# A two-block transformer kernel on one core: shorter first norm, other orders of weight splits, and another grouping of the second block's output projection

## What is computed

```python
def first_block(x, mem, ...):
    h = rms_norm(x, g[0])                       # the norm "n0"
    proj = h @ w_in[l]
    y_a = hyena_mixer(...); y_b = neighbourhood_attention(...); y_c = short_conv_mixer(...)
    merged = gates * (y @ w_branch) summed over the three
    x = x + rms_norm(merged @ w_out[l], g[1])   # residual "r1", then norm "n2"
    x = x + rms_norm(memory_cross_attention(...), g[3])        # "r3", then "n4"
    x = x + rms_norm(conv_glu_ffn(h, ffn_up, ffn_conv, ffn_down), g[5])   # "r5", then "n6"

def conv_glu_ffn(h, w_up, w_conv, w_down):
    u = dwconv3(h @ w_up, w_conv)
    g, val = jnp.split(u, 2, axis=-1)
    return (jax.nn.gelu(g, approximate=True) * val) @ w_down

def second_block(x, ...):
    y_a = mla_mixer(...)    # 6 heads, causal, latent queries and keys
    y_b = diff_mixer(...)   # 4 heads, p0 - lam * p1, then a norm over each head
    y_c = swa_mixer(...)    # 6 heads, window of 128
    h = h + jnp.concatenate([y_a, y_b, y_c], axis=-1) @ w_out[l]
    hn = rms_norm_2(h, ffn_norm[l])             # the norm "n8"
    h = h + (silu(hn @ w_gate[l]) * (hn @ w_up[l])) @ w_down[l]
    h = rms_norm_2(h, final_norm)
```

## Time and profile before

| | us |
|---|---|
| median of 3 runs | 1924.4 |
| lowest, highest | 1922.62, 1929.21 |
| the profiled execution, its own time | 1930.18 |
| its span, first to last instruction | 1928.4 |

### The profile page before, as it was taken

How to read it: one execution, slowest core, us unless ns; L and a number is a source line. 1 busy time by engine, 2 the same in 40 slices (tenths; PEclk the granted TensorE clock), 3 DMA queues, 4 the chain that set the end, 5 groups by cost and what they waited for, 6 DMA issues and landing times.

```text
span 1928.4 us, 22192 instructions
## 1 busy us (share of the span) xinstructions
PE 1825.9 (95%) x8955; PEld 1461.8 (76%) x8955; DVE 1016.3 (53%) x1521; ACT 733.0 (38%) x1219; POOL 289.0 (15%) x233
## 2 busy tenths in 40 slices
PE   7899999999999988989999999889978999999998
PEld 5678876788888866777888888777656778888887
DVE  6777844444454466357777722574354644444322
ACT  4433343332334444344344422444355632223221
POOL 1013501011212140141111100500100111111000
PEclk9899999999999999989999999898987999999999
DMA  5222322232224321222232232331210122222221
GB/s 187 84 80 88 110 77 77 77 110 98 95 91 164 132 87 34 72 71 77 88 104 93 77 109 99 107 102 52 79 42 32 45 87 99 98 88 99 92 94 55
DMA packets 49829, 171.13 MB, mean 89 GB/s; under 512 B 5882, under 2 KB 8570, under 8 KB 49600
## 3 DMA queue, kind: packets, MB, share of 16 engines
q1 hardware_dynamic: 45216, 155.69, 24.1%
q0 software_dynamic: 3936, 13.51, 2.1%
q10 hardware_dynamic: 576, 0.52, 0.1%
HBM read 165.51 MB, written 4.19 MB: 88 GB/s over the span
## 4 chain that ended last, share of the span: by engine, by line
PE 80%; DVE 8%; ACT 5%; issue 4%; POOL 2%; DMA 1%; SPq 0%; DVEq 0%; POOLq 0%; ACTq 0%
PE ps L373 25%; PE ps L375 24%; PE ps L374 24%; PE ps L378 3%; PE ps L2563 2%; ACT ws_h L301 1%; DVE ws_l L309 1%; POOL sums L420 1%; PE ps L2580 1%; ACT P L2687 1%; POOL x L1422 1%; DMA x<-in_x 1%; DVE tmp L800 0%; DVE P L2810 0%; ACT PT L2703 0%
## 5 line engine op out<-in xcount | busy, mean ns | idle before, releaser
L309 DVE TENSOR_TENSOR ws_l<-raw,ws_h 128x1024 fp32r<-128x1024 f32 x289 | 392.0, 1361 | 538.2 <-ACT ws_h L301 537.9
L373 PE MATMUL ps<-h_h,ws_h 128*128 128x512 f32 (+1 forms) x1448 | 584.8, 404 | 32.4 <-DVE ws_l L309 13.5
L374 PE MATMUL ps<-h_l,ws_h 128*128 128x512 f32 (+1 forms) x1448 | 573.9, 396 | 0.0
L375 PE MATMUL ps<-h_h,ws_l 128*128 128x512 f32 (+1 forms) x1448 | 573.6, 396 | 0.0
L301 ACT ACTIVATE ws_h<-raw 128x1024 fp32r<-128x1024 f32 x289 | 303.6, 1054 | 462.4 <-PE ps L375 458.4
L373 PEld LDWEIGHTS ps<-h_h,ws_h 128*128 128x128 f32 x1448 | 278.4, 192 | 108.1 <-issue 23.6
L375 PEld LDWEIGHTS ps<-h_h,ws_l 128*128 128x128 f32 x1448 | 278.9, 193 | 62.1
L374 PEld LDWEIGHTS ps<-h_l,ws_h 128*128 128x128 f32 x1448 | 279.8, 193 | 59.1 <-issue 0.2
L373 PE MATMUL ps<-G_h,ws_h 128*128 128x512 f32 (+1 forms) x374 | 143.0, 382 | 1.1 <-DVE ws_l L309 1.1
L375 PE MATMUL ps<-G_h,ws_l 128*128 128x512 f32 (+1 forms) x374 | 142.6, 381 | 0.0
L374 PE MATMUL ps<-G_l,ws_h 128*128 128x512 f32 (+1 forms) x374 | 142.6, 381 | 0.0
(11 more groups left out here) (437 smaller groups left out, 2425.3 us busy)
## 6 DMA issues: line engine op xcount, KB each, us to landing
raw<-in_ffn_up SPq DMA_DIRECT2D x88, 512.0 KB, 3.3
raw<-in_w_merge SPq DMA_DIRECT2D x36, 512.0 KB, 3.4
raw<-in_ffn_down SPq DMA_DIRECT2D x22, 512.0 KB, 3.4
raw<-in_w_down SPq DMA_DIRECT2D x22, 512.0 KB, 3.3
raw<-in_w_hy SPq DMA_DIRECT2D x12, 512.0 KB, 4.6
raw<-in_w_sc SPq DMA_DIRECT2D x12, 512.0 KB, 3.3
raw<-in_fwd SPq DMA_DIRECT2D x8, 512.0 KB, 3.4
raw<-in_w_naqk SPq DMA_DIRECT2D x8, 512.0 KB, 3.2
```

Source lines behind the costliest of these rows:

```text
L309: dve.e.tensor_tensor(w.lo, raw[n % NRAW][:], w.hi, ALU.subtract).then_inc(*lo_made.says(("lo", n)))
L373: pe.e.matmul(o, a.hi, b.hi, start=start, stop=False, skip_group_check=True)
L374: pe.e.matmul(o, a.hi, b.lo, start=False, stop=False, skip_group_check=True)
L375: return pe.e.matmul(o, a.lo, b.hi, start=False, stop=stop, skip_group_check=True)
```

## The change

It has these parts. (1) n0 uses the form with tokens over the partitions, and POOL adds all six squares; the spread stands on PE behind projection tile 3. (2) In `residual_dve` (r1, r3, r5) the low part of h tile 0 comes one tile sooner. (3) In both feed-forwards one chunk call moves from round 21 to the place between the evacuations of i = 0 and i = 1 in round 2, so that all rounds from 3 on run one chunk further ahead. (4) In `latent_*` the queries of each pair come ahead of its keys, and both ahead of the values; the eight small operations for lambda go to the start of the DVE's stage. (5) The output projection is grouped as k = 0, 1 (`pm`), k = 2, 3 (`pd`) and k = 4 to 7 (after the attention); `pm 0` may start once the last `turn` of M 2 is issued, `pd 0` once `mixed` of D 0 is. (6) `difference` of block 3 of a D pair moves ahead of the next pair's first scores. (7) `out2_*` follows the grouping: 32 blocks in place of 24, four h tiles made early in place of five.

By the planner's rule the D and W pairs get 32 dense steps of three matmuls in place of 40. `pm 0` to `pm 7` stand from the last `turn` of M 2 to the second scores of block 3 of D 1; `pd 0` behind `mixed` of D 0, and `pd 7` behind `over` of W 1, so that W 2 has none (before: `pd 0` behind `mixed` of D 1, `pd 7` behind `over` of W 2).

```diff
@@ -34,8 +34,8 @@
-LAST_PARTS = [(m, k) for m in range(3) for k in (5, 6)] + [(m, 7) for m in range(3)] + [
-    (m, k) for m in range(3, 8) for k in (5, 6, 7)]
+LAST_PARTS = [(m, k) for m in range(2) for k in (4, 5, 6)] + [(m, 7) for m in range(2)] + [
+    (m, k) for m in range(2, 8) for k in (4, 5, 6, 7)]
@@ -579,7 +579,9 @@
                 pe.wait_ge("consts")
-                total("n0", L, bank(("sum", "n0"), main), 8, True)
+                total_of_tokens("n0", bank(("sum", "n0"), main))
+            if m == 3:
+                spread_tokens("n0", bank(("spread", "n0"), main))
             if m == 5:
@@ -697,7 +699,9 @@
             if t == ("hy", 2):
-                root("n0", L, D, rh[:, 0:L])
+                root_of_tokens("n0", D)
+            if t == ("hy", 3):
+                scale_of_tokens("n0", rh[:, 0:L])
             if t == ("hy", 4):
@@ -756,8 +760,6 @@
         sine("f1", 64, 1, "hy_b1", "hy_f1", turns)
-        for m in (2, 4, 6):
-            add_square(dve, added_dve, "n0", m, L)
@@ -769,8 +771,8 @@
                     *dve_part.says(("H", 1)))
-            if t == ("hy", 3):
-                inverse("n0", rh[:, 0:L])
+            if t == ("hy", 2):
+                inverse_of_tokens("n0")
             if t == ("hy", 4):
@@ -904,7 +906,7 @@
         pool.e.dma_start(dec[:], A["decay"]).then_inc(*dec_in.says("dec", by=16))
-        for m in (1, 3, 5):
+        for m in range(1, 7):
             add_square(pool, added_pool, "n0", m, L)
@@ -1403,7 +1405,9 @@
                     *dve_out.says(("rs", v, m), ("off done", v) if off else ("free", (v, m))))
-            if m > 1:
+            if m == 1:
+                h_rest(nv, 0, ngain, dst(0))
+            elif m > 2:
                 h_rest(nv, m - 2, ngain, dst(m - 2))
@@ -1749,6 +1753,8 @@
+
+    UP_CHUNKS = [8, 16, 16] + [16] * 18 + [8, 0]
     UP_LATE = [[] if i < 2 else [0, 1] if i == 2 else [i - 1] for i in range(23)]
@@ -1767,13 +1773,14 @@
         for n in range(23):
-            f.next(8 if n == 0 else 16 if n < 22 else 0)
+            f.next(UP_CHUNKS[n])
             if n == 22:
...
             for i in UP_LATE[n]:
+                f.next(8 if i == 1 else 0)
                 for j in range(2):
@@ -1841,12 +1849,12 @@
     def out2_pe():
-        main, blocks = rings["main"], Blocks("w_out_w", 24)
+        main, blocks = rings["main"], Blocks("w_out_w", 32)
         for m, k in LAST_PARTS:
-            o = bank(("o2", m), main) if k == 5 else out_of(("o2", m))
+            o = bank(("o2", m), main) if k == 4 else out_of(("o2", m))
             w = blocks.next()
             pe.wait_ge(("mix", k))
-            i = mm(o, w, hk(k), k == 5, k == 7)
+            i = mm(o, w, hk(k), k == 4, k == 7)
             what = blocks.says() + ([("done", ("o2", m))] if k == 7 else [])
@@ -1867,11 +1875,11 @@
             squared_x(m)
-            if m < 5:
+            if m < 4:
                 begun(m)
-            if m in (1, 4):
+            if m in (1, 3, 5):
                 f.next(8)
-        for m in range(5, 8):
+        for m in range(4, 8):
             begun(m)
@@ -1879,7 +1887,7 @@
-        return ("done", ("pm", 7) if m < 3 else ("pd", 7) if m < 5 else ("o2", 7))
+        return ("done", ("pm", 7) if m < 2 else ("pd", 7) if m < 4 else ("o2", 7))
@@ -1892,11 +1900,11 @@
             onto_x("o2", m, ("x", "o2", m), ("x", "pd", m))
-            if 1 < m < 7:
+            if 1 < m < 6:
                 h_rest("n8", m - 2, "ffn_norm_2", hm(m - 2))
-            if m in (1, 4):
+            if m in (1, 3, 5):
                 f.next(8)
-        for m in range(5, 8):
+        for m in range(4, 8):
             h_rest("n8", m, "ffn_norm_2", hm(m))
@@ -2091,20 +2101,19 @@
             keys_pe(("dk", m), dblocks)
-        rings["dense"] = dblocks, Blocks("w_swa", 32), Blocks("w_qb", 12), Blocks("w_out_m", 24), Blocks("w_out_d", 16)
+        rings["dense"] = dblocks, Blocks("w_swa", 32), Blocks("w_qb", 12), Blocks("w_out_m", 16), Blocks("w_out_d", 16)
         n = chunk_pe("w_kvb")
         for p in range(2):
+            for t in ("qn", "qr"):
+                o = bank((t, p), main)
+                for k in range(2):
+                    query_part(t, p, k, o)
             for i in range(2):
...
                True).then_inc(*products.says(("done", ("vl", i)), over(n) if i == 4 else None))
-        for p in range(2):
-            for t in ("qn", "qr"):
-                o = bank((t, p), main)
-                for k in range(2):
-                    query_part(t, p, k, o)
@@ -2215,7 +2224,10 @@
         act.e.activation(KW.hi, wsp[n % NSPLIT][:, 0:384].hi, ACT.Copy).then_inc(*act_part.says("KW hi"))
+        fq.next(8)
         for p in range(2):
+            query_hi2("qn", p)
+            query_hi2("qr", p)
             for i in range(2):
@@ -2223,10 +2235,6 @@
                 *act_out.says(("V made2", i), ("free", ("vl", i))))
-        fq.next(8)
-        for p in range(2):
-            query_hi2("qn", p)
-            query_hi2("qr", p)
         act.wait_ge("lam sums")
@@ -2241,6 +2249,17 @@
     def latent_dve():
+        pl = PCOL["lam"]
+        for i in range(2):
+            a, b = small[:, 16 + 16 * i:32 + 16 * i], small[:, 48:64]
+            at = lambda q: par[:, pl + 64 * i + 16 * q:pl + 64 * i + 16 * q + 16]
+            dve.e.tensor_tensor(a, at(0), at(2), ALU.mult).then_inc(*dve_part.says(("lam a", i)))
+            dve.wait_ge(("lam s", i - 1) if i else None)
+            dve.e.tensor_tensor(b, at(1), at(3), ALU.mult).then_inc(*dve_part.says(("lam b", i)))
+            dve.wait_ge(("lam a", i), ("lam b", i))
+            dve.e.tensor_tensor(a, a, b, ALU.add).then_inc(*dve_part.says(("lam s", i)))
+            dve.wait_ge(("lam s", i))
+            dve.e.tensor_reduce(small[:, 2 + i:3 + i], a, AX.X, ALU.add).then_inc(*dve_part.says("lam sums"))
         f = Follow(chunk_dve)
@@ -2294,25 +2313,13 @@
         dve.e.tensor_scalar(KW.lo, wsp[n % NSPLIT][:, 0:384].lo, 1.0, None, ALU.mult).then_inc(*dve_part.says("KW lo"))
-        for p in range(2):
-            for i in range(2):
-                key_lo(p, i)
         fq.next(8)
...
             query_lo2("qr", p)
...
+            for i in range(2):
+                key_lo(p, i)
         dve.wait_ge("lam exp")
@@ -2402,7 +2409,7 @@
     def steps_of(t):
-        return {"sk": 8, "q2": 8, "kn": 1, "qn": 2, "qr": 2, "pm": 3, "pd": 2}[t[0]]
+        return {"sk": 8, "q2": 8, "kn": 1, "qn": 2, "qr": 2, "pm": 2, "pd": 2}[t[0]]
@@ -2468,9 +2475,9 @@
                     break
-                if t == ("pm", 0) and ("mixed", ("M", 2), None) not in said:
+                if t == ("pm", 0) and ("turn", ("M", 2, 3), "meta") not in said:
                     break
-                if t == ("pd", 0) and ("mixed", ("D", 1), None) not in said:
+                if t == ("pd", 0) and ("mixed", ("D", 0), None) not in said:
                     break
@@ -2493,7 +2500,7 @@
                 before = STEPS[at - 1][1]
-                if at and before[0] == "D" and STEPS[at][1] != before:
+                if at and before[0] == "D" and before[2] < 3 and STEPS[at][1] != before:
                     yield "difference", before, None
@@ -2504,6 +2511,8 @@
                 yield "over", u[0:2], None
+            if u[2] == 2 and u[0] == "D":
+                yield "difference", u[0:2] + (3,), None
             if n:
@@ -2631,7 +2640,7 @@
                 blocks = {"q2": dblocks if m < 2 else sblocks, "pm": mblocks, "pd": oblocks}[t[0]]
-                kk = k + (3 if t[0] == "pd" else 0)
+                kk = k + (2 if t[0] == "pd" else 0)
                 if t[0] != "q2":
@@ -3112,8 +3121,8 @@
     wo = wo.reshape(8, 128, 8, 128).transpose(2, 0, 1, 3)
-    A["w_out_m"] = chunks_of(wo[:, 0:3].reshape(-1, 128, 128))
-    A["w_out_d"] = chunks_of(wo[:, 3:5].reshape(-1, 128, 128))
+    A["w_out_m"] = chunks_of(wo[:, 0:2].reshape(-1, 128, 128))
+    A["w_out_d"] = chunks_of(wo[:, 2:4].reshape(-1, 128, 128))
     A["w_out_w"] = chunks_of(np.stack([wo[m, k] for m, k in LAST_PARTS]))
...
     A["ffn_up_2"] = blocks_of(up)
```

20 lines of the change are left out of this document (6 added, 14 removed).

## The result

The changed kernel takes 1917.8 us (median of 20 runs, 1911.2 to 1922.9), the kernel before, on the same chip, 1927.7 us. The ratio is 0.9942 with an interval of 0.9931 to 0.9953, that is -11.2 us (-13.3 to -9.1). It is faster, by about half of the -23.7 us that were forecast. 1917.8 lies inside the stated range of 1888 to 1920, near its slow end; the forecast was 1900.7. The profiled execution took 1918.88 us, its span is 1917.1.

The account below looks back on a forecast made before the run. PE (TensorE), busy 1825.9 of 1928.4 us, bounds the kernel, so only its waits and half-clock stretches count. The terms sum to -23.7 us: 1906.5 us profiled, median 5.8 us below, so 1900.7 us, range 1888 to 1920.

Parts of the forecast that it names:

- (f): Attention: 20 us lost to half clock; 0.3 of it taken back with the longest waits gone; -6, between -12 and 0.
- Part 1: First norm: first tile scaled at 43.4 in place of 45.64, POOL adding all squares; -2.0, between -3.3 and -0.5.
- part 2: r1, r3, r5: low part of first h tile comes sooner, PE waits less; -1.0, between -1.9 and +0.8.
- the first norm doesn't do what it says: Rival: PE's two tiles hold the spread, POOL is slow, first norm at +1, total 1903.7 us; chance 0.05.
- Part 3: First feed-forward, round 2: earlier chunk removes a 4.30 us stall and its clock loss; -7.0, between -7.8 and -3.0.
- Part 4: Latent stage: queries come first, so scores start about 1.3 us sooner; -1.3, between -3.0 and +0.5.
- (b): Attention: two turns wait 7.1 us for difference; the first wait goes whole, 1.8 us of the second stays; -5.3.
- (d): Attention: new wait, DVE stands at pm 0's add until x returns; +2.6, between 0 and +4.
- (a): Attention: pm 0 no longer needs mix 2, for which it waited 4.3 us; -4.3.
- (e): Attention: 8 blocks, 5.6 us, move behind it, half of that counted as cost; +2.8, between 0 and 5.6.
- part 6: End of output projection: PE's 2.2 us wait for a split goes, as DVE keeps up; -2.4, between -2.6 and 0.
- the attention gives nothing: Rival: attention at zero: x's return delays exps, less filler keeps clock down, moved blocks lie bare; 1910.7 us, chance 0.22.

Follow-up runs that it names:

- e1: Kernel before with the change's first norm alone (sum by tokens, POOL adding all six squares): 1929.8 us, ratio 1.0013.
- e2: Kernel before with the chunk call between the evacuations of the two feed-forwards alone: 1925.7 us, ratio 0.9990.
- e11: Kernel before with the reordered latent stage alone (queries ahead of keys and values, lambda's small operations earlier): 1925.5 us, ratio 0.9974.
- e5: Kernel before with the new place of the differences and the regrouped output projection, nothing else: 1922.0 us, ratio 0.9967.
- e4: Kernel before with the new place of the last difference of each D pair alone: 1915.35 us, ratio 0.9935.
- e10: Kernel before with the first norm's sum by tokens, its squares still added by DVE and POOL in turns: 1926.0 us, ratio 0.9985.
- e17: Kernel before with new place of differences and regrouped projection, but M's products starting only behind mixed M 2: 1916.2 us, ratio 0.9946.
- e18: Kernel before with new place of differences and 8 blocks moved behind the attention (M over 3 tiles, D over 1): 1915.2 us, ratio 0.9953.
- e6: Changed kernel with the regrouping of the projection taken back, all other edits kept: 1916.6 us, ratio to the kernel before 0.9937.
- e7: Changed kernel without the regrouping and with the first norm's squares added in turns: 1909.6 us, ratio to the kernel before 0.9904.
- e15: Second measurement of the changed kernel without regrouping, first norm's squares added in turns: 1907.1 us, ratio to the kernel before 0.9904.
- e12: Changed kernel with M over 2 tiles, D over 3, 24 blocks behind, first norm's squares added in turns: 1910.4 us, ratio to before 0.9904.
- after: First measurement and trace of the changed kernel, all edits against the kernel before: 1917.8 us, ratio 0.9942.
- e13: The changed kernel once more, unchanged, with a new profile: 1917.0 us, ratio to the kernel before 0.9957.

## Why the prediction was wrong

The parts as forecast and as measured, alone or in pairs:

| part | forecast | measured | by |
|---|---|---|---|
| 1 first norm | -2.0 | +2.5 (-1.2 to +6.2) | e1 |
| 2 low part sooner | -1.0 | about -0.2 in waits | traces |
| 3 feed-forwards | -7.0 | -1.9 (-5.2 to +1.3) | e2 |
| 4 latent | -1.3 | -5.0 (-8.1 to -1.9) | e11 |
| 5 and 6 attention, projection | -12.4 | -6.4 (-9.8 to -2.9) | e5 |
| sum | -23.7 | -11.0 | change: -11.2 |

**The step that failed first: the clock.** In part 5 it is (f), "with the longest waits gone I take back 0.3 of it, -6". The waits went (28.5 to 21.9 us idle in the last stage), and PE's busy time there rose by 6.1 us. Without (f), parts 5 and 6 forecast -4.3 - 5.3 + 2.6 + 2.8 - 2.4 = -6.6 us, and the idle time fell by 6.5. That the two agree so well is partly luck, as the single terms below show. Over the whole kernel 9.4 us were taken from the clock, and PE's busy time did not move (1825.9 and 1825.8): what the last stage lost, other stages won, r1 to r3 among them, for which nothing was forecast. Over many executions a little came: the mean granted clock is 0.970 over the 20 runs of the changed kernel, and 0.967 to 0.969 over those of the kernel before beside the single edits. When a single edit did bring clock (e4, 5.9 us; e11, about 4), nothing in my sum had said which one would. Why the clock comes with some edits and not with others stays open.

**Part 1: the wrong engine was watched.** POOL was done at 27.68 (forecast 27.5 to 29.6). The first tile came 4.3 us later than forecast (47.65 against 43.4). Of these, 1.2 us are in the start of the total, which stands behind the second sine product on PE (29.75 against 28.6), 1.7 us in the total and 1.2 in the two tiles, both at half clock in part, and 0.2 us in the rest. The failed step is "behind POOL's adds nothing waits", and the sentence that DVE is merely rid of work. I priced POOL's adds "beside a busy DVE" at 1.79 us in place of 1.29 and charged POOL alone, while the earlier trace rows shows DVE paying too. The lock was even named in part 2, with its price of 0.6 us per operation, but only as a smaller gain, whose 1.5 us come from no sum: the low ends of parts 1 and 2 as stated are -0.5 and +0.8. And without the lock, in e10, the first tile was at 45.43, so the term was too large by 2 us in any case. The rival that the first norm doesn't do what it says had a chance of 0.05 and the right sign, for reasons that were not the cause.

**Part 2: the lock took it back.** PE's three waits for the first low part of h sum to 9.4 us where they were 9.6 (waits of the kernel before for L536). At r3 the wait is 4.83 us where it was 4.73. The low part does start 0.5 us sooner behind the split ahead of it, but POOL's first add now starts just before it:

```profile
826.55 1.79 DVE L536 SCALAR_TENSOR_TENSOR h_l<-x,par,h_h 128x512 fp32r<-128x512 f32 x1
...
826.53 1.26 POOL L1426 TENSOR_TENSOR x<-x,tmp 128x512 f32<-128x512 f32 x1 [9.98 <-DVE tmp L1405]
```

It takes 1.79 us in place of 1.32 and ends as long behind the split as before (5.19 us, and 5.20 before). The failed step is "starts at about 832.05 and ends at 833.4": it took the old length, and the new place lies wholly behind POOL's add. The edit was not run alone, since 1 us is below what a run resolves.

**Part 3: the end of the chain.** The stall of 4.30 us and its 6.8 us at half clock went, as forecast. The new wait was looked for one chunk later (0.8 us) and came 200 us later, at the first output that needs all of G: 2.8 us. The failed step is "so DVE catches up", with no term for the end of the chain: DVE's slack per round is real for the splits, but the last tiles of G leave the chain when DVE's, ACT's and POOL's work on them is done, and the stall had only given them time. At its own place the forecast was right to the tenth, 7.0 us (e2), but by luck: the 0.8 us for the next chunk didn't come, and the clock gave 2.7 us and not 3.4. It was priced for 6.8 us at half clock, of which 1.4 lie in the wait itself (half clock from 886.9, the wait ends at 888.25). With the 3.2 us given back, the stage of this pair of traces gains 4.1 us, and over all traces 2.7.

**Part 4: the mechanism was right, its size was off.** The term of 1.3 us was for the start of the scores alone, and that start came 2.2 us sooner. The rest of the stage's 6 us is clock, which had no term in it.

**Parts 5 and 6: (f) failed, (b) was undone by (d), and (a) was no gain.** That -12.4 is also what the difference alone gave (-12.5) is luck, since it was the sum for seven terms. (b), -5.3, was right for the difference alone (7.1 us of waits to 1.7), but in the changed kernel 5.3 of the 7.1 us stay, and 5.0 in e5. (a), -4.3 for mix 2, was not a gain: where it was the only thing left (e4), the stage was faster than with it gone (e5). (d) named the right wait and the right queue, but its sum was too small: "DVE stands until then" was 0.71 us of waiting for x in the changed kernel, but a split of 1.23 us and its wait for ACT stand there too, so the reciprocal was 4.4 us late (e5 against e17) where 4.0 were forecast. What it costs is not only PE's wait for it, +2.6: it makes the differences late too, and e5 has 1.5 us more idle time and 6.0 us more busy time than e17. (e), the moved blocks at +2.8, and part 6, the end of the projection at -2.4, nearly cancel as forecast: e18 needs 1.5 us more than e4 from D's scores to the end, and neither the changed kernel nor e5 has the 2.2 us wait of the earlier trace rows. (Part 6 names four low parts and counts three; with four its sum is 6.1 us and not 5.3, above the 5.6 of PE, and yet no wait came.) For the changed kernel as a whole the rival "the attention gives nothing", at 0.22, is what its trace showed: 532.8 of 533.2 us. Of its reasons the low clock and the return of x are in the traces, the bare blocks are not; that less filler is what kept the clock down, no run shows (e6, with the old filler, has 59 us at half clock in that stage, e11 72).

The signs to look for came out so: no wait in 873 to 884 and a clock of 1.00 (right), the waits for `difference` 5.3 us (forecast: near 2), none for mix 2 (right), no wait ahead of the second feed-forward's third chunk (right), 43.4 for the first tile (47.65), 3 us of DVE idle ahead of the first add onto x (0.71). A clock under 0.8 in the D pairs was to be the sign that something is wrong, and it was 0.74.

## What to carry to other kernels

Forecast idle time and clock apart, and compare them apart: span less PE's busy time gives the one, busy time for the same matmuls the other. Here the idle time of the attention came out as forecast, and the clock that was to come with it did not. Work moved from DVE to POOL is not gone from DVE: in a stretch where both read SBUF, price the blocked steps of the one that PE waits for, and try adds with gaps in place of adds in a row. A stall taken out of a chain can come back at the chain's end (here 3 of 7 us), so look for the first operation that needs the last link. Where PE often idles, price first what a newly placed product pushes back on DVE's queue, and time the edits of one stage one by one and together.

The version that beats both kernels is all edits, with the adds of the first norm in turns and the old grouping, or D over three tiles: -18.5 us each (e7, e15, e12), against -11.2 for the change. The late start of M's products with the new grouping (e17) was not run together with the other edits.

## What was not expected of the hardware

- The time of one kernel varies by 7 to 19 us between its runs where there are eleven or more (1911.2 to 1922.9 for the changed one), and it goes with the granted clock. Over the 294 runs of this study that list their clock, within a kernel and chip, 0.001 of mean clock (some 3.8 us at half clock) goes with 1.3 us of time: 0.33 us per microsecond at half clock, not the half that a fully busy PE would lose.
- The same work at the same place can be at 1.2 or at 2.4 GHz in two executions of one kernel: from r1 to r3, 10 us and 20 us at half clock (after, e13), and 2.8 us of time. The Trainium skill says so of one kernel's first matmuls (TensorE: Matmul & The Clock Gate, section "Part 1: The HAM clock gate (the "warmup" mystery)"): how many run at the lower clock differs from run to run. The trace agrees, and shows it in the middle of a kernel too.
- Waits of about 1.4 and 1.9 us at the same matmul stood ahead of no and of 10.2 us at half clock (e7, e6).
- A DVE operation that started 0.02 us behind a POOL add of 1.26 us took 1.79 us, where the same form takes 0.75 us alone (at 16.48 in the changed kernel).
